# Attention weights times values: split fp32r products for two of four groups of key blocks, and another division of the column work between GpSimd and VectorE

## The chip, the cores and the metric

One core of a Trainium2 chip runs the whole program. The time is the device time of one execution in microseconds (us). TensorE (PE in the rows), VectorE (DVE), ScalarE (ACT), GpSimd (POOL) and the DMA queue of SyncE (SP) each work through an instruction list of their own, in order, and wait for each other on semaphores.

## What is computed

A two-layer encoder for 2048 prompt tokens and 256 sample tokens, width 1024, all in float32. Layer 0 is differential attention with 8 heads; layer 1 mixes by Fourier transforms. The change lies in layer 0, whose core is, for each head and each block of 128 queries:

```
s  = einsum(q, k) * scale - slope * |qpos - kpos|      # two maps m = 0, 1 per head, 2048 keys
p  = softmax(s)
pd = p[map 0] - lam * p[map 1]
o  = pd @ v                                            # v: 2048 keys x 128 columns
```

The 256 sample tokens attend among themselves in the same way.

## The kernel before

The program runs in stages: input projection, `attend`, output projection, then the three stages of the Fourier layer. `attend` is the second and longest one.

**Steps.** `attend` goes through 8 heads, and each head through 17 steps: q = 0 to 15 are the 16 blocks of 128 queries of the prompt, q = 16 is the sample. Every engine's list is written out by hand by its own `step(h, hs, q)`. A step of TensorE is: `half(0)`, `half(1)`, `turn(0)`, `pair(0)`, `turn(1)`, `half(2)`, `pair(1)`, `turn(2)`, `half(3)`, `turn(3)`, `pair(2)`, `pair(3)`.

**Scores.** `half(j)` writes 1024 columns of scores (map j // 2, half j % 2) to PSUM with fp32r matmuls (L1051, L1055, and L1054 for the diagonal block). Three score buffers (RING = 3) go round, so `half(1)` of a step waits for the exponential `exp(2)` of the step before. VectorE takes the maximum of each half (`maximum`, L1285) and, when both halves of a map are done, the scaled negative (`negative`, L1291). ScalarE then writes exp(scale * s - max) to `p0` (map 0) or `p1` (map 1) and the row sums (L1209).

**Combining.** One step later the two maps of a block become one set of weights, in place in `p0`. VectorE adds and inverts the row sums (`inverse_sums`, L1309 and L1312). GpSimd scales columns 0 to 1023 of `p1` by -lam / sum (L1377, signals `p1_scaled`), then columns 1024 to 2047 of `p1` (L1380), then the same columns of `p0` by 1 / sum (L1382), and adds the two (L1385, signals `weights_rest`). VectorE does columns 0 to 1023 with one instruction of two SBUF inputs (`combine`, L1323, signals `weights`); it stands last in VectorE's step.

**Turning.** A further step later `turn(c)` transposes 4 of the 16 key blocks of the weights (group c, 512 columns) with TensorE into the one PSUM buffer `turned` (L1085). ScalarE copies it to `wt` (`take_weights`, L1187), and the next `turn` waits for that copy. In steps 1 to 5 of a head there is a fifth turn, `turn_value` (L1094), for a part of v; it stands between `pair(2)` and `pair(3)`.

**Products.** `pair(x)` issues about a quarter of the step's products `vv[k] x wt[k]` (L1111), each 128 x 128 by 256 queries in float32; the trace shows each as two matmul instructions. A table (`QUARTERS`) spreads the 128 products of a head plus 2 of the sample over the 17 steps, in the order of k: 8 a step in most, two to each `pair`.

Of the kernel before, what the change touches and what calls it, by code (L numbers as in the profile page):

```python
# [60 lines left out]
def f32(ap):  # L61
    return ap.bitcast(F32)
# [720 lines left out]
def attend(nc, qk_hi, qk_lo, v_dram, o_dram, consts, lam_vectors, copies, first, rows, subln, ahead, ahead_branch, ahead_gate):  # L783
# [10 lines left out]
    SHORT, T0 = S_SAMPLE, S_PROMPT  # L794
    SCORES = 4 * NB + 2
    OUTS = NP + 1
    assert SCORES % RING == 0
    with ExitStack() as stack:
        m = Memory(nc, stack, "pa")

        ka = [first["ka"], m.sb("ka1", [P, 2, S], F32R)]
        kb = [[first["kb"], m.sb("kb01", [HD + ALIBI, S], F32R)],
              [m.sb(f"kb1{n}", [HD + ALIBI, S], F32R) for n in range(2)]]
        qa = [first["qa"], m.sb("qa1", [P, 2, PAIR], F32R)]
# [3 lines left out]
        vv = m.sb("vv", [P, NB + 2, P])  # L808
        p0 = m.sb("p0", [P, 4, S])
        p1 = m.sb("p1", [P, 2, S])  # L810
        wt = m.sb("wt", [P, 2, NB, PAIR])
# [23 lines left out]
        sq = m.sb("sq", [P, 2, 2, GROUP])  # L835
        row_w = m.sb("row_w", [P, 1])
        eps = m.sb("eps", [P, 1])
# [23 lines left out]
        turned_out = m.sem("turned_out")  # L861
# [6 lines left out]
        lam = load_lambda(m, m.sem("lam_in"))  # L868
# [70 lines left out]
        with nc.Block() as block:  # L939
            @block.sync  # L940
            def _(sp):
# [20 lines left out]
                def load_sample(h):  # L962
# [6 lines left out]
                    sp.dma_start(f32(diag_s[:]), row(consts["diag"], h, 0, P, 0, P)).then_inc(sample_in, 16)  # L969
# [64 lines left out]
            def _(pe):  # L1034
# [24 lines left out]
                def score_sample(h, n):  # L1059
                    no = 4 * NB + n  # L1060
                    if n == 0:
                        pe.wait_ge(sample_in, 144 * (h + 1))
                    wait(pe, exps, SCORES * h + no - RING + 1)
                    for b in range(2):
# [3 lines left out]
                        pe.matmul(out[:, at], ident_r[:], diag_s[:], start=False, stop=False)  # L1068
# [3 lines left out]
                def turn_weights(h, t, c):  # L1072
# [24 lines left out]
                def pair_product(h, q, quarter):  # L1097
                    for g, k, back in products_of[q][quarter]:
# [1744 lines left out]
```

## Time and profile before

| | us |
|---|---|
| median of 3 runs (2963.0 to 2968.81) | 2967.51 |
| the profiled execution's own time | 2963.53 |
| its span, first to last instruction | 2961.7 |
| mean granted TensorE clock | 0.981 |
| TensorE matmul busy, over the span | 2828.0 (95%) |
| VectorE, ScalarE, GpSimd busy | 1808.4, 1742.0, 1550.8 |
| in 1200 to 1400 us, inside `attend`: TensorE busy | 197.94 of 200 |
| the same stretch: VectorE, ScalarE, GpSimd busy | 144.58, 149.94, 124.87 |

The profile is one execution. `attend` runs from about 780 to 2050 us. Busy times of matmuls overlap, because matmuls are pipelined: what a matmul costs is the distance from its start to the next one's start. Idle time of an engine matters only where another engine waits at its end.

### The profile page before, as it was taken

The page shows a single profiled execution, that of the slowest core. Times are in us where ns is not written, and L with a number is a line of the kernel's source. Part 1 is how long each engine was busy: PE and PEld are TensorE (multiplying, and loading weights), DVE is VectorE, ACT ScalarE, POOL GpSimd, SP SyncE. Part 2 cuts the span into 40 slices and gives each one's busy share as a digit, 9 for nine tenths or more (in the row PEclk, how much of TensorE's full clock was granted, in tenths as well). Part 3 has the DMA queues.
Part 4 walks back from the last instruction along what each step waited for, and adds up shares of the span by engine and source line. Part 5 has one row for each costly group of instructions (what it writes and reads, how often), then busy time and mean ns, then how long its engine had stood idle before and what let it go on. Part 6 is the DMA issues. An engine that isn't in the chain of part 4 may idle for free. (4 is left out here: it accounts for less than half of the span.)

```text
span 2961.7 us, 41608 instructions
## 1 busy us (share of the span) xinstructions
PE 2828.0 (95%) x15126; PEld 2485.1 (84%) x15126; DVE 1808.4 (61%) x2402; ACT 1742.0 (59%) x3126; POOL 1550.8 (52%) x988
## 2 busy tenths in 40 slices
PE   5999999999799999999999999998999899899898
PEld 4999999999688787878788888886788899886687
DVE  7678668766576767777777777776886200441322
ACT  6777777767477777777777777775443311322321
POOL 4566655655366666666565666666664320230642
PEclk8999999999999999999999999999999999999899
DMA  3664554447452314141414131122565522565752
GB/s 113 186 198 136 175 172 149 151 145 205 125 178 77 95 29 107 36 109 36 106 31 109 36 88 56 31 91 87 193 206 174 176 90 78 159 171 197 257 193 99
DMA packets 281815, 374.02 MB, mean 126 GB/s; under 512 B 22923, under 2 KB 258507, under 8 KB 276140
## 3 DMA queue, kind: packets, MB, share of 16 engines
q1 hardware_dynamic: 281484, 371.23, 40.8%
q8 instruction: 121, 1.98, 0.3%
q14 instruction: 82, 0.67, 0.1%
q0 software_dynamic: 128, 0.13, 0.0%
HBM read 258.04 MB, written 125.97 MB: 130 GB/s over the span
## 5 line engine op out<-in xcount | busy, mean ns | idle before, releaser
L1285 DVE TENSOR_REDUCE pa_half_max<-pa_score 128x1 f32<-128x1024 f32 x512 | 623.9, 1219 | 322.6 <-PE pa_score L1055 322.5
L1209 ACT ACTIVATE pa_p<-pa_score,pa_neg_max 128x1024 f32<-128x1024 f32 x512 | 567.3, 1110 | 66.8 <-DVE pa_neg_max L1291 66.7
L1111 PE MATMUL pa_o_acc<-pa_wt,pa_vv 128*128 128x256 f32 x2048 | 513.9, 380 | 1.5 <-ACT pa_o_out_s L1248 1.5
L206 PE MATMUL ia_acc<-ia_xh,ia_wh 128*128 128x384 f32 x1344 | 454.3, 338 | 33.3 <-DVE ia_xl L675 15.9
L451 POOL TENSOR_TENSOR ia_w_sums<-ia_raw 128x512 f32<-128x512 f32 x240 | 334.1, 1395 | 256.2 <-PE ia_acc L208 236.3
L1051 PE MATMUL pa_score<-pa_ka,pa_qa 128*128 128x512 f32 x1024 | 453.0, 442 | 15.0 <-ACT pa_p L1209 8.0
L207 PE MATMUL ia_acc<-ia_xl,ia_wh 128*128 128x384 f32 x1344 | 452.3, 337 | 0.0
L208 PE MATMUL ia_acc<-ia_xh,ia_wl 128*128 128x384 f32 x1344 | 452.2, 336 | 0.0
L1187 ACT ACTIVATE pa_wt<-pa_turned 128x512 f32<-128x512 f32 x512 | 305.9, 597 | 241.7 <-PE pa_turned L1085 236.8
L1055 PE MATMUL pa_score<-pa_kb,pa_qb 96*128 96x512 f32 x1024 | 420.8, 411 | 0.0
L1111 PEld LDWEIGHTS pa_o_acc<-pa_wt,pa_vv 128*128 128x128 f32 x2048 | 366.2, 190 | 44.8 <-ACT pa_o_out_s L1248 3.1
L1377 POOL TENSOR_SCALAR pa_p<-pa_p,pa_inv_sum,pa_lam_neg 128x1024 f32<-128x1024 f32 x128 | 153.1, 1196 | 447.2 <-DVE pa_inv_sum L1312 447.2
L695 DVE TENSOR_TENSOR ia_c<-ia_c,ia_acc 128x384 f32<-128x384 f32 x384 | 199.0, 549 | 199.1 <-PE ia_acc L208 181.1
L1085 PE MATMUL pa_turned<-pa_ident,pa_p 128*128 128x128 f32 x2048 | 313.1, 275 | 3.9 <-ACT pa_wt L1187 3.6
L1385 POOL TENSOR_TENSOR pa_p<-pa_p 128x1024 f32<-128x1024 f32 x128 | 302.5, 2363 | 23.8 <-POOL pa_p L1382 23.8
L1085 PEld LDWEIGHTS pa_turned<-pa_ident,pa_p 128*128 128x128 f32 x2048 | 243.3, 140 | 77.6 <-ACT pa_wt L1187 39.4
L206 PEld LDWEIGHTS ia_acc<-ia_xh,ia_wh 128*128 128x128 f32 x1344 | 254.9, 190 | 39.2 <-issue 38.7
L207 PEld LDWEIGHTS ia_acc<-ia_xl,ia_wh 128*128 128x128 f32 x1344 | 254.7, 190 | 0.3
L208 PEld LDWEIGHTS ia_acc<-ia_xh,ia_wl 128*128 128x128 f32 x1344 | 254.8, 190 | 0.0
L1051 PEld LDWEIGHTS pa_score<-pa_ka,pa_qa 128*128 128x128 f32 x1024 | 195.5, 191 | 54.0 <-ACT pa_p L1209 14.9
L659 DVE TENSOR_TENSOR ia_wl<-ia_acc,ia_wh 128x512 fp32r<-128x512 f32 x336 | 225.8, 681 | 3.6 <-ACT ia_acc L565 3.1
L1055 PEld LDWEIGHTS pa_score<-pa_kb,pa_qb 96*128 96x128 f32 x1024 | 195.9, 191 | 33.4
(286 smaller groups left out, 5236.9 us busy)
## 6 DMA issues: line engine op xcount, KB each, us to landing
ia_raw<-attn_w_in SPq DMA_DIRECT2D x48, 1024.0 KB, 6.3
qk_hi<-ia_hi SPq DMA_DIRECT2D x96, 192.0 KB, 5.0
qk_lo<-ia_c SPq DMA_DIRECT2D x96, 192.0 KB, 3.0
pa_ka<-qk_hi SPq DMA_DIRECT2D x32, 512.0 KB, 9.0
fl_slices<-normed SPq DMA_DIRECT2D x26, 512.0 KB, 6.5
ia_h<-x_cols SPq DMA_DIRECT2D x24, 384.0 KB, 4.2
v<-ia_c SPq DMA_DIRECT2D x48, 192.0 KB, 5.6
attn_gate<-ia_c SPq DMA_DIRECT2D x48, 192.0 KB, 2.0
```

The costliest lines, as they stand in the source:

```text
L206: pe.matmul(out, a_hi(k), b_hi(k), start=first and n == 0, stop=False)
L207: pe.matmul(out, a_hi(k), b_lo(k), start=False, stop=False)
L208: mm = pe.matmul(out, a_lo(k), b_hi(k), start=False, stop=last and n == len(ks) - 1)
L451: pool.tensor_tensor(w_sums[:, s % RING], x, y, op).then_inc(w_sum, 1)
L1051: pe.matmul(out[:, c], qa[s][:, n, at:at + P], ka[hs][:, n, cols], start=True, stop=False)
L1055: mm = pe.matmul(out[:, c], qb[s][:, n, at:at + P], kb[hs][n][:, cols], start=False, stop=True)
L1085: mm = pe.transpose(turned[:, x * P:(x + 1) * P], src, ident[:])
L1111: mm = pe.matmul(acc, vv[:, k], wt[:, g % 2, k], start=k == 0, stop=k == NB - 1)
L1187: act.activation(wt[:, s, 4 * c:4 * c + 4, at:at + P], turned[:].rearrange("p (k t) -> p k t", k=4), ACT.Copy).then_inc(turned_out, 1)
L1209: act.activation(dst[:, half * HALF:(half + 1) * HALF], score[:, (4 * q + j) % RING].rearrange("p a b -> p (a b)"), ACT.Exp, bias=neg_max[ ...
L1285: dve.tensor_reduce(half_max[:, q % 2, n, half:half + 1], score[:, (4 * q + j) % RING].rearrange("p a b -> p (a b)"), AX_X, ALU.max).then_ ...
L1385: pool.tensor_tensor(b, b, p1[:, par, HALF:], ALU.add).then_inc(weights_rest, 1)
```

## The change

In `attend`, the key blocks of groups 1 and 3 (`LOW = (1, 3)`, 8 of the 16 blocks) no longer use one float32 product. Their turned weights and values are kept as a high part in fp32r and a remainder: `wt_hi`, `wt_lo`, `vv_hi`, `vv_lo`. Each product of such a block becomes three fp32r matmuls (hi x hi, hi x lo, lo x hi). ScalarE's copy writes the high part, as long as before; VectorE writes the remainder with a new instruction (`weights_low`, `v_low`: `turned` minus the high part, 512 columns, read from PSUM and SBUF). The next `turn` waits for this too (`low_out`), as `turned` is read twice.

The combining is divided anew: VectorE joins columns 0 to 511, GpSimd the other 1536. `combine` moves up in VectorE's step, behind `negative` of the first map, with `weights_low(1)` behind it; `weights_low(3)` and `v_low` stand last. `turn(1)` now waits for GpSimd's part, as `turn(2)` did, and so does `exp(2)` where `exp(3)` did. `turn_value` moves behind `pair(3)`. The sample's diagonal table is no longer loaded apart (8 small DMAs fewer), and some small buffers share memory.

```diff
@@ turn_weights, on TensorE
-                    if c == 2:
+                    if c == 1:
                         pe.wait_ge(weights_rest, NB * h + t - 1 if t >= 2 else NB * h)
                     wait(pe, turned_out, unit(h, t, "w", c))
+                    wait(pe, low_out, lows(h, t, "w", c))
@@ pair_product, on TensorE
-                            mm = pe.matmul(acc, vv[:, k], wt[:, g % 2, k], start=k == 0, stop=k == NB - 1)
+                            if is_low(k):
+                                at = low_at(k)
+                                pe.matmul(acc, vv_hi[:, at], wt_hi[:, g % 2, at], start=False, stop=False)
+                                pe.matmul(acc, vv_hi[:, at], wt_lo[:, g % 2, at], start=False, stop=False)
+                                mm = pe.matmul(acc, vv_lo[:, at], wt_hi[:, g % 2, at], start=False, stop=k == NB - 1)
+                            else:
+                                mm = pe.matmul(acc, vv[:, full_at(k)], wt[:, g % 2, full_at(k)], start=k == 0, stop=False)
@@ step, on TensorE
-                        turn_value(q - 1)
                         pair(3)
+                        turn_value(q - 1)
@@ exponential, on ScalarE
-                    if j == 3 and not (is_first(h) and q < 2):
+                    if j == 2 and not (is_first(h) and q < 2):
                         act.wait_ge(weights_rest, NB * h + (q - 1 if q >= 1 else -1))
@@ combine and the new instructions, on VectorE
-                    a, par = p0[:, (q - 1) % 4, :HALF], (q - 1) % 2
-                    dve.scalar_tensor_tensor(out=a, in0=a, scalar=inv_sum[:, par, 0:1], in1=p1[:, par, :HALF],
+                    a, par = p0[:, (q - 1) % 4, :GROUP], (q - 1) % 2
+                    dve.scalar_tensor_tensor(out=a, in0=a, scalar=inv_sum[:, par, 0:1], in1=p1[:, par, :GROUP],
                                              op0=ALU.mult, op1=ALU.add).then_inc(weights, 1)
+                def weights_low(h, t, c):
+                    dve.wait_ge(turned_out, unit(h, t, "w", c) + 1)
...
+                    dve.tensor_tensor(wt_lo[:, s, ks, at:at + P], turned[:].rearrange("p (k t) -> p k t", k=4),
+                                      f32(wt_hi[:, s, ks, at:at + P]), ALU.subtract).then_inc(low_out, 1)
@@ step, on VectorE
                             maximum(h, q, 1)
                             negative(h, q, 0)
+                        if parts["before"]:
+                            combine(h, q)
+                        low(1)
+                        if parts["score"]:
                             maximum(h, q, 2)
                             maximum(h, q, 3)
                             negative(h, q, 1)
-                    if parts["before"]:
-                        combine(h, q)
+                    low(3)
+                    if parts["score"] and (q, "v", q - 1) in place and q - 1 in LOW:
+                        v_low(h, q, q - 1)
@@ step, on GpSimd (HALF is 1024 columns, GROUP 512)
-                    pool.tensor_scalar(p1[:, par, :HALF], p1[:, par, :HALF], inv_sum[:, par, 1:2], lam["neg"][:, 0:1],
+                    pool.tensor_scalar(p1[:, par, :GROUP], p1[:, par, :GROUP], inv_sum[:, par, 1:2], lam["neg"][:, 0:1],
                                        ALU.mult, ALU.mult).then_inc(p1_scaled, 1)
-                    b = p0[:, (q - 1) % 4, HALF:]
-                    pool.tensor_scalar(p1[:, par, HALF:], p1[:, par, HALF:], inv_sum[:, par, 1:2], lam["neg"][:, 0:1],
+                    b = p0[:, (q - 1) % 4, GROUP:]
+                    pool.tensor_scalar(p1[:, par, GROUP:], p1[:, par, GROUP:], inv_sum[:, par, 1:2], lam["neg"][:, 0:1],
                                        ALU.mult, ALU.mult).then_inc(p1_rest, 1)
...
-                    pool.tensor_tensor(b, b, p1[:, par, HALF:], ALU.add).then_inc(weights_rest, 1)
+                    pool.tensor_tensor(b, b, p1[:, par, GROUP:], ALU.add).then_inc(weights_rest, 1)
```

VectorE's order in one step in the middle of a head, from the maximum of the first score half on. Before (x2 means twice in a row):

```order
L1285 TENSOR_REDUCE pa_half_max<-pa_score 128x1
L1309 TENSOR_TENSOR pa_row_sum<-pa_half_sum 128x2
L1312 RECIPROCAL pa_inv_sum<-pa_row_sum 128x2
L1285 TENSOR_REDUCE pa_half_max<-pa_score 128x1
L1291 TENSOR_SCALAR pa_neg_max<-pa_half_max 128x1
L1285 TENSOR_REDUCE pa_half_max<-pa_score 128x1 x2
L1291 TENSOR_SCALAR pa_neg_max<-pa_half_max 128x1
L1323 SCALAR_TENSOR_TENSOR pa_p<-pa_p,pa_inv_sum 128x1024
```

and now, where L1322, L1346, L1349, L1328 and L1360 are the former L1285, L1309, L1312, L1291 and L1323:

```order
L1322 TENSOR_REDUCE pa_half_max<-pa_score 128x1
L1346 TENSOR_TENSOR pa_row_sum<-pa_half_sum 128x2
L1349 RECIPROCAL pa_inv_sum<-pa_row_sum 128x2
L1322 TENSOR_REDUCE pa_half_max<-pa_score 128x1
L1328 TENSOR_SCALAR pa_neg_max<-pa_half_max 128x1
L1360 SCALAR_TENSOR_TENSOR pa_p<-pa_p,pa_inv_sum 128x512
L1368 TENSOR_TENSOR pa_wt_lo<-pa_turned,pa_wt_hi 128x4x128
L1322 TENSOR_REDUCE pa_half_max<-pa_score 128x1 x2
L1328 TENSOR_SCALAR pa_neg_max<-pa_half_max 128x1
L1368 TENSOR_TENSOR pa_wt_lo<-pa_turned,pa_wt_hi 128x4x128
```

The combining instruction, half as wide, has moved from the end to a place ahead of the two maxima of the second map; a remainder instruction (L1368) follows it, and another ends the step.

TensorE's order at the end of step q = 2, from `turn(3)` to the first score matmul of the next step. Before:

```order
L1085 MATMUL pa_turned<-pa_ident,pa_p 128x128 x4
L1111 MATMUL pa_o_acc<-pa_wt,pa_vv 128x256
L1094 MATMUL pa_turned<-pa_ident,pa_vt 128x128 x4
L1111 MATMUL pa_o_acc<-pa_wt,pa_vv 128x256
L1051 MATMUL pa_score<-pa_ka,pa_qa_51 128x512
```

and now (L1112 and L1122 are the former L1085 and L1094, L1077 the former L1051):

```order
L1112 MATMUL pa_turned<-pa_ident,pa_p 128x128 x4
L1143 MATMUL pa_o_acc<-pa_wt_hi,pa_vv_hi 128x256
L1144 MATMUL pa_o_acc<-pa_wt_lo,pa_vv_hi 128x256
L1145 MATMUL pa_o_acc<-pa_wt_hi,pa_vv_lo 128x256
L1143 MATMUL pa_o_acc<-pa_wt_hi,pa_vv_hi 128x256
L1144 MATMUL pa_o_acc<-pa_wt_lo,pa_vv_hi 128x256
L1145 MATMUL pa_o_acc<-pa_wt_hi,pa_vv_lo 128x256
L1122 MATMUL pa_turned<-pa_ident,pa_vt 128x128 x4
L1077 MATMUL pa_score<-pa_ka,pa_qa 128x512
```

The two products of this place, both of group 3, have become three matmuls each, and the turn of the values stands behind both instead of between them.

## Rows read from the trace of the kernel before

**Rows 1.** Timeline of one step: start, duration in us, engine, line [idle before, releaser].
```profile
1213.82 0.58 PE L1051 MATMUL pa_score<-pa_ka,pa_qa 128*128 128x512 f32 x1
...
1214.56 0.19 ACT L1209 ACTIVATION_READ_ACCUMULATOR pa_p<-pa_score,pa_neg_max 128x1 f32 x1
...
1214.80 0.19 PEld L1051 LDWEIGHTS pa_score<-pa_ka,pa_qa 128*128 128x128 f32 x1
...
1216.85 1.20 POOL L1377 TENSOR_SCALAR pa_p<-pa_p,pa_inv_sum,pa_lam_neg 128x1024 f32<-128x1024 f32 x1 [3.12 <-DVE pa_inv_sum L1312]
1217.27 0.42 PEld L1085 LDWEIGHTS pa_turned<-pa_ident,pa_p 128*128 128x128 f32 x4 [0.22 <-ACT pa_wt L1187]
...
1217.79 0.22 DVE L1291 TENSOR_SCALAR pa_neg_max<-pa_half_max 128x1 f32<-128x1 f32 x1
1217.97 0.60 ACT L1187 ACTIVATE pa_wt<-pa_turned 128x512 f32<-128x512 f32 x1 [0.75 <-PE pa_turned L1085]
...
1218.92 1.23 DVE L1285 TENSOR_REDUCE pa_half_max<-pa_score 128x1 f32<-128x1024 f32 x1 [0.91 <-PE pa_score L1055]
...
1219.37 0.57 PEld L1085 LDWEIGHTS pa_turned<-pa_ident,pa_p 128*128 128x128 f32 x4
...
1220.77 0.45 PE L1055 MATMUL pa_score<-pa_kb,pa_qb 96*128 96x512 f32 x1
...
1221.50 1.89 PE L1111 MATMUL pa_o_acc<-pa_wt,pa_vv 128*128 128x256 f32 x8
...
1222.52 0.21 DVE L1291 TENSOR_SCALAR pa_neg_max<-pa_half_max 128x1 f32<-128x1 f32 x1
...
1222.76 1.11 ACT L1209 ACTIVATE pa_p<-pa_score,pa_neg_max 128x1024 f32<-128x1024 f32 x1 [0.37 <-DVE pa_neg_max L1291]
...
1223.04 0.58 PE L1051 MATMUL pa_score<-pa_ka,pa_qa 128*128 128x512 f32 x1
```
**Rows 2.** Timeline, Fourier stage: first and twelfth of twelve fp32r matmuls of 256 columns.
```profile
2578.08 0.28 PE L206 MATMUL fl_ps<-fl_asn 128*128 128x256 f32 x1
...
2579.38 0.28 PE L208 MATMUL fl_ps<-fl_asn 128*128 128x256 f32 x1
```
**Rows 3.** Timeline, GpSimd and VectorE side by side in steps 16 and 1 of a head.
```profile
932.55 1.20 POOL L1377 TENSOR_SCALAR pa_p<-pa_p,pa_inv_sum,pa_lam_neg 128x1024 f32<-128x1024 f32 x1 [2.73 <-DVE pa_inv_sum L1312]
...
933.30 0.47 DVE L1299 TENSOR_SCALAR pa_neg_s<-pa_max_s 128x2 f32<-128x2 f32 x1
933.73 2.24 POOL L1380 TENSOR_SCALAR pa_p<-pa_p,pa_inv_sum,pa_lam_neg 128x1024 f32<-128x1024 f32 x1
933.78 1.28 DVE L1323 SCALAR_TENSOR_TENSOR pa_p<-pa_p,pa_inv_sum 128x1024 f32<-128x1024 f32 x1
...
953.55 2.35 POOL L1385 TENSOR_TENSOR pa_p<-pa_p 128x1024 f32<-128x1024 f32 x1 [0.18 <-POOL pa_p L1382]
...
954.88 2.11 DVE L1323 SCALAR_TENSOR_TENSOR pa_p<-pa_p,pa_inv_sum 128x1024 f32<-128x1024 f32 x1
```
**Rows 4.** Timeline, output projection: two VectorE and two GpSimd additions, all from SBUF.
```profile
2057.51 5.85 DVE L1806 TENSOR_TENSOR oa_wl<-oa_raw,oa_wh 128x1024 fp32r<-128x1024 f32 x2 [2.07 <-ACT oa_wh L1741]
...
2058.92 6.67 POOL L1596 TENSOR_TENSOR oa_wl<-oa_raw,oa_wh 128x1024 fp32r<-128x1024 f32 x2
```
**Rows 5.** Timeline of the first stage, then ns (min/median/max) of two lines of `attend`.
```profile
42.51 2.11 DVE L659 TENSOR_TENSOR ia_wl<-ia_acc,ia_wh 128x512 fp32r<-128x512 f32 x3
...
42.67 3.44 POOL L466 TENSOR_TENSOR ia_x_sums<-ia_hi,ia_h 128x1536 f32<-128x1536 f32 x1 [22.30 <-DVE ia_h L671]
...
L1318 DVE SCALAR_TENSOR_TENSOR pa_p_s<-pa_p_s,pa_inv_s x16: 475/478/483, 946.3 to 2032.4; 128x256 f32<-128x256 f32 x16
...
L1372 POOL TENSOR_SCALAR pa_p_s<-pa_p_s,pa_inv_s,pa_lam_neg x16: 550/554/556, 940.4 to 2031.4; 128x256 f32<-128x256 f32 x16
```
**Rows 6.** Timeline of TensorE: `turn_value` in steps 2 and 3 of a head.
```profile
963.99 0.66 PE L1094 MATMUL pa_turned<-pa_ident,pa_vt 128*128 128x128 f32 x4 [0.46 <-ACT pa_wt L1187]
...
973.47 0.66 PE L1094 MATMUL pa_turned<-pa_ident,pa_vt 128*128 128x128 f32 x4 [0.89 <-ACT pa_wt L1187]
```

More of the change, by code:

```diff
@@ L794, in attend @@
     SHORT, T0 = S_SAMPLE, S_PROMPT
+    LOW = (1, 3)
+    LOW_NB = 4 * len(LOW)
     SCORES = 4 * NB + 2
@@ L807, in attend @@
         vt = m.sb("vt", [P, T])
-        vv = m.sb("vv", [P, NB + 2, P])
+        vv = m.sb("vv", [P, NB + 2 - LOW_NB, P])
+        vv_hi = m.sb("vv_hi", [P, LOW_NB, P], F32R)
+        vv_lo = m.sb("vv_lo", [P, LOW_NB, P], F32R)
         p0 = m.sb("p0", [P, 4, S])
         p1 = m.sb("p1", [P, 2, S])
-        wt = m.sb("wt", [P, 2, NB, PAIR])
+        wt = m.sb("wt", [P, 2, NB - LOW_NB, PAIR])
+        wt_hi = m.sb("wt_hi", [P, 2, LOW_NB, PAIR], F32R)
+        wt_lo = m.sb("wt_lo", [P, 2, LOW_NB, PAIR], F32R)
         o_out = m.sb("o_out", [P, 2, PAIR])
@@ L834, in attend @@
         ones = m.sb("ones", [P, P])
-        sq = m.sb("sq", [P, 2, 2, GROUP])
-        row_w = m.sb("row_w", [P, 1])
-        eps = m.sb("eps", [P, 1])
+        small = m.sb("small", [P, 3])
+        row_w, eps = small[:, 0:1], small[:, 1:2]
         score = m.ps("score", [P, RING, 2, GROUP])
@@ L867, in attend @@
         pool_held, sp_held = m.sem("pool_held"), m.sem("sp_held")
-        lam = load_lambda(m, m.sem("lam_in"))
+        lam = load_lambda(m, m.sem("lam_in"), p_s_at, small[:, 2:3])
         order = []
@@ L881, in unit, with lows, is_low, full_at @@
             return UNITS * h + place[(t, kind, c)] - SKIPPED
+        low_order = [x for x in order if x[2] in LOW]
+        LOWS = len(low_order)
+        SKIPPED_LOWS = len(LOW)
+        def lows(h, t, kind, c):
+            return LOWS * h + sum(place[x] < place[(t, kind, c)] for x in low_order) - SKIPPED_LOWS
+        def is_low(k):
+            return k // 4 in LOW
+        def full_at(k):
+            return sum(not is_low(x) for x in range(k))
+        def low_at(k):
+            return sum(is_low(x) for x in range(k))
         def turned_block(t):
@@ L1067, in score_sample @@
                         pe.matmul(out, qa_s[:, n, at], ka_s[:, n], start=True, stop=False)
-                        pe.matmul(out[:, at], ident_r[:], diag_s[:], start=False, stop=False)
+                        pe.matmul(out[:, at], ident_r[:], diag[1][:], start=False, stop=False)
                         mm = pe.matmul(out, qb_s[:, n, at], kb_s[:, n], start=False, stop=True)
@@ L1091, in turn_v @@
                     wait(pe, turned_out, unit(h, t, "v", c))
+                    wait(pe, low_out, lows(h, t, "v", c))
                     for x in range(4 if c < NC else 2):
@@ L1104, in pair_product @@
                                 pe.wait_ge(turned_out, unit(h, 1, "w", 0) + 1)
-                            mm = pe.matmul(acc, vv[:, NB + k], wt_s[:, k], start=k == 0, stop=k == 1)
+                            mm = pe.matmul(acc, vv[:, full_at(NB + k)], wt_s[:, k], start=k == 0, stop=k == 1)
                         else:
@@ L1166, in step @@
                         pair(2)
+                        pair(3)
                         turn_value(q - 1)
-                        pair(3)
                     if is_last(h) and q == SAMPLE:
@@ L1339, in step @@
                             negative(h, q, 0)
+                        if parts["before"]:
+                            combine(h, q)
+                        low(1)
+                        if parts["score"]:
                             maximum(h, q, 2)
```

44 lines of the change are left out of this document (31 added, 13 removed).

## The prediction

> **What bounds the kernel now.** I read the page first: TensorE is 95% busy over the span, and the table by stretches gives it 197.94 of 200 us inside `attend`. A shorter product looks like a gain there. So I then walked through one step in the timeline [rows 1]. It lasts from the first score matmul at 1213.82 to the next at 1223.04: 9.22 us. Two chains run round in it, and the reader should see that both are full.
>
> The first is TensorE's own work, end to end. The second goes through the other engines. The last matmul of `half(3)` ends at 1221.22 (1220.77 + 0.45). VectorE's maximum of that half follows it, then the negative (1222.52 to 1222.73), and the exponential `exp(2)` (from 1222.76). The same exponential one step earlier ends with its accumulator read at 1214.75, and the weight load of `half(1)` starts at 1214.80. `half(1)` is thus released just in time. From there TensorE goes through `turn(0)`, `pair(0)`, `turn(1)`, `half(2)`, `pair(1)`, `turn(2)` and `half(3)`, and the ring is closed. Within it `turn(1)` waits as well: its weight load at 1217.27 has 0.22 us of idle ahead, ended by ScalarE's copy of `turn(0)`.
>
> **The products.** A float32 product is two matmuls: eight of them take 1.89 us [rows 1], which is (1.89 - 0.38) / 7 = 0.216 us apiece, or 0.432 for a product. Fp32r matmuls of 256 columns follow each other by (2579.38 - 2578.08) / 11 = 0.118 us [rows 2]; three make 0.354. A split product saves 0.078 us. There are 8 blocks x 8 pairs x 8 heads = 512 of them: 40 us of TensorE.
>
> By the table `QUARTERS` the split products of steps 5 to 14 lie in `pair(0)` and `pair(3)`, two in each. What `pair(0)` saves (0.16 us) is lost to `turn(1)`, which waits for the copy anyway. What `pair(3)` saves lies before `half(1)`, which is held by `exp(2)`: `half(0)` starts 0.16 us sooner, and `half(1)` waits. Hardly any of the 40 us reaches the end: the second ring has only the 0.05 us between 1214.75 and 1214.80 in it, and that is signal time. I take 0.
>
> **What is added to the second ring.** `turn(2)` must now wait for VectorE's remainder of `turn(1)`, which stands behind `combine`. When does `combine` run?
>
> GpSimd starts at 1216.85 [rows 1]. Its scaling takes 0.554 us for 256 columns [rows 5] and 1.20 for 1024 [rows 3], so 0.84 ns a column: 0.77 for 512 and 1.63 for 1536. It signals `p1_scaled` at 1217.62 and goes straight on with the 1536 columns, until 1219.25. VectorE finishes the negative at 1218.01 [rows 1] and comes to `combine` in the midst of this.
>
> Rows 3 show what happens then. The `combine` at 954.88 takes 2.11 us: GpSimd's addition runs until 955.90 (953.55 + 2.35), and `combine` ends 1.09 us later, at 956.99. In steps in which it starts clear of GpSimd it takes 1.28. At 933.78 it is the other way round: `combine` comes 0.05 us after a GpSimd scaling has begun, takes its normal 1.28 us, and the scaling takes 2.24 instead of 1.20. So the two exclude each other, and the later one waits for the whole instruction of the other. A small VectorE instruction at 933.30 lasts 0.47 us, until 933.77, and GpSimd's scaling ends at 933.75; a scaling excludes as well. Today `combine` stands last in the step, when GpSimd is nearly through and TensorE is not waiting.
>
> What the rows don't hold is a `combine` that begins in the middle of a scaling. The Trainium skill, page "SBUF — State Buffer", section "SBUF: two separate sides", covers it: a VectorE instruction with two SBUF inputs and a GpSimd instruction that reads SBUF share one port pair, an exclusive lock held for the whole instruction. By that rule the sum is the one below, 3080 us; if one held that a scaling lets `combine` in, it would be 2983. The trace agrees with the rule in all three places of rows 3.
>
> So `combine` gets going at 1219.25. A 512-column one is 0.53 us shorter than the 1.09, by (1.28 - 0.478) / 768 = 1.04 ns a column [rows 3, 5]: it ends at 1219.81. Does GpSimd's next queued scaling get in first? The nearest case is in the output projection: two VectorE additions (5.85 us) and two of GpSimd (6.67 us) started 1.41 us apart and went by turns [rows 4]; so one instruction is waited for, not two. The remainder takes 2.11 / 3 = 0.70 us, like the instruction of the first stage that also reads PSUM and SBUF; it ran beside a GpSimd addition of 3.44 us without being stretched [rows 5], so it needs no turn. ScalarE's copy, its input, is there at 1218.57 [rows 1]. It ends near 1220.42, and `turn(2)` loads weights at 1220.46. Today it loads at 1219.37 and could have done so about 0.15 later without loss: **0.95 us late**. As `half(0)` comes 0.16 us earlier than now, GpSimd's start moves with it, and 0.80 is left in steps 6 to 15. `half(3)`, the maximum, `exp(2)` and the next `half(1)` all move by this.
>
> Bounds: without exclusion `combine` ends at 1218.7 and the remainder at 1219.4, 0 late. With both scalings ahead of it, 1.63 later than mine. Within my case, scaling at a fixed rate per column (0.60 and 1.80 us) or a different spacing moves it by 0.15 either way.
>
> **Other edits.** GpSimd's additions of 1536 columns take 3.44 us [rows 5]; its step is 0.77 + 1.63 + 0.56 + 1.63 + 0.2 + 3.44 = 8.2 us of about 10, and its part arrives near 1225.1, before `turn(1)` at about 1227. No wait. `exp(2)`'s earlier wait is met likewise. `maximum(2)` starts up to 1.4 us later than 1218.92, but must only be done before `half(3)` is. The 8 sample DMAs fewer are behind other work: 0.
>
> `turn_value` (steps 1 to 5) now waits for the remainder of `turn(3)`, which stands behind the second negative. Today the wait is for ScalarE's copy alone: 0.46 us in step 2, 0.89 in step 3 [rows 6]. In steps 2 to 5 it starts 2.3 us after `half(3)` ends (0.04 + 1.22 + 0.25 for maximum and negative, 0.70 remainder, signals) instead of 1.4, less the product now ahead of it: 0.44, 0.95, 0.44, 0.46, together 2.3 us a head. In these four steps `half(0)` is not early, so the full 0.95 applies. Step 16: between `turn(1)` and `turn(2)` stand only the three products of `pair(2)`, two of them split (0.432 + 2 x 0.354 = 1.1 us), against copy plus remainder (1.4 us with signals): 0.3. Step 0: `combine` of the sample waits for GpSimd's longer addition: 0.4. Step 1: no `turn(1)`, four split products: -0.2.
>
> **The sum.** Per head 10 x 0.80 + 4 x 0.95 + 2.3 + 0.3 + 0.4 - 0.2 = 14.6 us; eight heads: 117. On the profiled execution's own 2963.5 us this is **3080**; it lies 4 us under the median shown, within the spread of the three runs.
>
> **Rivals.**
> - *Nothing blocks `combine`.* Then only the `turn_value` steps, step 16 and step 1 count: 2.4 x 8 = 19, so 2983 (2975 to 2990). Against it stand rows 3. Chance 0.09.
> - *Faster: the product saving arrives.* If `exp(2)` in truth leaves `half(1)` room, or the ring re-forms around TensorE, up to 40 us come through: 2923, or 2942 with the `turn_value` costs. It decides at a ring slack of more than 0.2 us a step; the 0.05 of rows 1 speaks against it, as does the copy wait at `turn(1)`. Chance 0.06.
> - *`combine` waits for both scalings.* Another 1.63 us in 14 steps, 8 heads: +180, so 3260. Rows 4 speak against it. Chance 0.04.
> - *The change doesn't shorten products* (a three-matmul product costs more than 0.354 because its weight loads show). Rows 2 have the same three-matmul form with a load each; and the ring would hide it. No case of its own.
>
> **How the numbers follow.** Main case 0.79, own range 3050 to 3115 (0.15 us x 14 x 8 = 17 us on either side, and as much again for the special steps). To leave out no more than 2 in 10 the range reaches down to the first rival: 2980 to 3115. A measurement of this kernel tells about 0.2% from no change, 6 us. Slower by more: main, first and third rival, 0.92; faster by more, the second, 0.06; within 0.2%: 0.02, where saving and waits cancel.
>
> **What would show it.** In a middle step, `combine` (512 columns) lasting about 1.8 us and ending 0.56 after a GpSimd scaling of 1536 columns; `turn(2)`'s weight load waiting for VectorE's remainder, some 0.8 to 1.0 us, over 100 times; a step of 10.0 us; products of split blocks 0.118 us apart; VectorE's remainders at 0.70 us. If `combine` takes 0.75 us and the step is still 9.2, the exclusion was misread. If the step is under 9.1, the second ring was.

## The result and the profile after

| | before | after |
|---|---|---|
| median, us | 2967.25 (2963.0 to 2968.81, 4 runs) | 3090.66 (3087.16 to 3094.91, 4 runs) |
| ratio to before, 95% interval | | 1.0418 [1.0406, 1.0431] |
| span of the profiled execution | 2961.7 | 3088.0 |
| VectorE busy | 1808.4 | 1998.5 |
| GpSimd busy | 1550.8 | 1797.0 |
| one step in the middle of a head | 9.22 | 10.04 |
| one head, median of the seven distances between heads | 155.8 | 169.9 |

The change costs 123.4 us. The last two rows are distances between starts of GpSimd's first scaling (L1377 before, L1439 after), which runs once in each step but that after the sample.

The table by stretches of the kernel after gives, for the same 200 us as in the table of before, the busy time of each engine, then granted clock, DMA share and GB/s:

```profile
core 0: us, PE busy (x) PEld busy (x) DVE busy (x) ACT busy (x) POOL busy (x), PEclk, DMA share, GB/s
1200.00:1400.00 200.00, 183.47 (x1073) 151.06 (x1072) 161.11 (x222) 137.62 (x254) 151.31 (x79) 1.00 0.22 60
```

TensorE was busy 197.94 of these 200 us, now 183.47, with the clock at full: it waits. The waits inside `attend` (engine, tile, line, what released it: us in total, times, longest) say for what. "issue" stands for idle time that no recorded event ended:

```profile
PEld pa_turned L1112 <- issue: 151.6, 238, 2.7
PE pa_turned L1112 <- DVE pa_wt_lo L1368: 82.7, 116, 2.3
...
PE pa_turned L1122 <- DVE pa_wt_lo L1368: 34.9, 32, 1.8
```

The turns wait for VectorE's remainder, `turn(2)` once in nearly every step and `turn_value` four times a head. The timeline of one middle step (start, duration, engine, line, [idle before, releaser]) answers to [rows 1]:

```profile
1409.99 0.77 POOL L1439 TENSOR_SCALAR pa_p<-pa_p,pa_inv_sum,pa_small 128x512 f32<-128x512 f32 x1 [1.96 <-DVE pa_inv_sum L1349]
...
1410.73 1.63 POOL L1442 TENSOR_SCALAR pa_p<-pa_p,pa_inv_sum,pa_small 128x1536 f32<-128x1536 f32 x1
1410.93 0.21 DVE L1328 TENSOR_SCALAR pa_neg_max<-pa_half_max 128x1 f32<-128x1 f32 x1
...
1411.06 1.84 DVE L1360 SCALAR_TENSOR_TENSOR pa_p<-pa_p,pa_inv_sum 128x512 f32<-128x512 f32 x1
...
1411.27 0.60 ACT L1225 ACTIVATE pa_wt_hi<-pa_turned 128x512 fp32r<-128x512 f32 x1 [0.76 <-PE pa_turned L1112]
...
1412.34 2.06 POOL L1444 TENSOR_SCALAR pa_p<-pa_p,pa_inv_sum,pa_ones 128x1536 f32<-128x1536 f32 x1
...
1412.82 0.68 DVE L1368 TENSOR_TENSOR pa_wt_lo<-pa_turned,pa_wt_hi 128x512 fp32r<-128x512 f32 x1
1413.42 1.21 DVE L1322 TENSOR_REDUCE pa_half_max<-pa_score 128x1 f32<-128x1024 f32 x1
1413.62 0.42 PEld L1112 LDWEIGHTS pa_turned<-pa_ident,pa_p 128*128 128x128 f32 x4 [0.99 <-issue]
1413.65 0.63 PE L1112 MATMUL pa_turned<-pa_ident,pa_p 128*128 128x128 f32 x4 [0.62 <-DVE pa_wt_lo L1368]
```

Read it from the middle. `combine` (L1360) starts at 1411.06, 0.33 us into GpSimd's scaling of 1536 columns, and lasts 1.84 us: it ends at 1412.90, 0.54 after the scaling (1410.73 + 1.63 = 1412.36). GpSimd's next scaling starts then too and takes 2.06 instead of 1.63: it waits in its turn. The copy of `turn(1)` (L1225) is there at 1411.87, but its remainder (L1368) runs only from 1412.82, and `turn(2)` loads weights at 1413.62 after 0.99 us of idle. In [rows 1] it loaded them 1.58 us after the negative started, now 2.69. This is nearly every step. The page's group (count | busy in all, mean ns | idle before) has a mean of 1.76 us, and of its 128 instructions 119 wait for GpSimd:

```profile
L1360 DVE SCALAR_TENSOR_TENSOR pa_p<-pa_p,pa_inv_sum 128x512 f32<-128x512 f32 x128 | 225.3, 1760 | 1.1 <-POOL pa_p L1439 1.1
```

### The profile page after: what moved, and what is told of

Its sections match the earlier page's. It is cut to its first block and busy times, and to the rows that moved or that the text cites. A ratio compares the mean times of both kernels' runs of the same rounds, so it can differ in the third digit from the quotient of the medians.

```text
span 3088.0 us, 43186 instructions
## 1 busy us (share of the span) xinstructions
PE 2841.8 (92%) x15638; PEld 2484.9 (80%) x15638; DVE 1998.5 (65%) x2674; ACT 1746.1 (57%) x3126; POOL 1797.0 (58%) x988
## 5 line engine op out<-in xcount | busy, mean ns | idle before, releaser
L1322 DVE TENSOR_REDUCE pa_half_max<-pa_score 128x1 f32<-128x1024 f32 x512 | 621.3, 1215 | 193.8 <-PE pa_score L1081 193.8
L1077 PE MATMUL pa_score<-pa_ka,pa_qa 128*128 128x512 f32 x1024 | 445.8, 435 | 14.3 <-ACT pa_p L1246 9.2
L1447 POOL TENSOR_TENSOR pa_p<-pa_p 128x1536 f32<-128x1536 f32 x128 | 444.9, 3476 | 23.8 <-POOL pa_p L1444 23.8
L1112 PE MATMUL pa_turned<-pa_ident,pa_p 128*128 128x128 f32 x2048 | 316.8, 277 | 89.5 <-DVE pa_wt_lo L1368 84.9
L1112 PEld LDWEIGHTS pa_turned<-pa_ident,pa_p 128*128 128x128 f32 x2048 | 234.7, 141 | 190.9 <-issue 152.4
L1225 ACT ACTIVATE pa_wt<-pa_turned 128x512 f32<-128x512 f32 x256 | 153.3, 599 | 279.3 <-PE pa_turned L1112 278.9
L1439 POOL TENSOR_SCALAR pa_p<-pa_p,pa_inv_sum,pa_small 128x512 f32<-128x512 f32 x128 | 98.3, 768 | 325.7 <-DVE pa_inv_sum L1349 325.7
L1147 PE MATMUL pa_o_acc<-pa_wt,pa_vv 128*128 128x256 f32 x1024 | 263.7, 380 | 0.0
L1444 POOL TENSOR_SCALAR pa_p<-pa_p,pa_inv_sum,pa_ones 128x1536 f32<-128x1536 f32 x128 | 259.6, 2028 | 0.0
L1077 PEld LDWEIGHTS pa_score<-pa_ka,pa_qa 128*128 128x128 f32 x1024 | 197.0, 192 | 62.7 <-ACT pa_p L1246 38.1
L1360 DVE SCALAR_TENSOR_TENSOR pa_p<-pa_p,pa_inv_sum 128x512 f32<-128x512 f32 x128 | 225.3, 1760 | 1.1 <-POOL pa_p L1439 1.1
```

What stands on the lines that cost most here:

```text
L1077: pe.matmul(out[:, c], qa[s][:, n, at:at + P], ka[hs][:, n, cols], start=True, stop=False)
L1112: mm = pe.transpose(turned[:, x * P:(x + 1) * P], src, ident[:])
L1147: mm = pe.matmul(acc, vv[:, full_at(k)], wt[:, g % 2, full_at(k)], start=k == 0, stop=False)
L1322: dve.tensor_reduce(half_max[:, q % 2, n, half:half + 1], score[:, (4 * q + j) % RING].rearrange("p a b -> p (a b)"), AX_X, ALU.max).then_ ...
L1444: pool.tensor_scalar(b, b, inv_sum[:, par, 0:1], ones[:, 0:1], ALU.mult, ALU.mult).then_inc(p0_rest, 1)
L1447: pool.tensor_tensor(b, b, p1[:, par, GROUP:], ALU.add).then_inc(weights_rest, 1)
```

## Experiments

Each ratio is to the kernel before on the same chip. Lengths of steps are read as above.

### Each part alone

`only_split`, against the kernel after (the waits for GpSimd's part go back to `turn(2)` and `exp(3)` as well):

```diff
-                        if parts["before"]:
-                            combine(h, q)
                         low(1)
...
                     low(3)
+                    if q != SAMPLE and parts["before"]:
+                        combine(h, q)
@@ combine and GpSimd: HALF for GROUP throughout
-                    a, par = p0[:, (q - 1) % 4, :GROUP], (q - 1) % 2
+                    a, par = p0[:, (q - 1) % 4, :HALF], (q - 1) % 2
...
-                    b = p0[:, (q - 1) % 4, GROUP:]
+                    b = p0[:, (q - 1) % 4, HALF:]
```

> One part alone: the split products, with their remainders on VectorE, the high parts from ScalarE, the sample's weights and the turn of v behind pair(3) as in the change; the division of the columns (1024 and 1024), the combining instruction at the end of VectorE's step and the waits of turn(2) and exp(3) are those of the kernel before. The remainder of turn(1) then stands directly behind the first negative, with nothing queued ahead of it that GpSimd can block. Theory: the remainders alone cost nothing in a middle step (0.68 us on VectorE, ended 0.1 us before turn(2) would start anyway), so the step stays at 9.22 to 9.35 us; the turns of v still cost their 2.3 us a head and the last stage of attend some 8 us, which makes 2967 + 18 + 8 = about 2990. Rival 1: the 40 us of cheaper products count as soon as the combining instruction is out of the way: 2950. Rival 2: the remainders and waits are dear by themselves, whatever stands behind the negative: 3050 or more.

Measured: 2998.7 us, 1.0107 [1.0092, 1.0122], 9 above the expectation. The middle step is 9.19; steps 2 to 5 take 10.95, 10.69, 11.61 and 9.18 in the second head, where the kernel before takes 9.27, 9.21, 9.80 and 9.70. So the remainders are free in a middle step. The excess lies at the turns of v, and part of it is TensorE's clock. In this head TensorE waits 1.82 us for a turn of v, until 980.96, and then its granted clock falls from 1.00 to about 0.5 (2.4 to 1.2 GHz) for 3.5 us. The third-last number of each row is the granted clock:

```profile
core 0: us, PE busy (x) PEld busy (x) DVE busy (x) ACT busy (x) POOL busy (x), PEclk, DMA share, GB/s
976.00:981.00 5.00, 3.18 (x19) 2.46 (x19) 4.13 (x7) 4.19 (x8) 4.82 (x4) 1.00 0.45 110
981.00:984.50 3.50, 3.50 (x11) 3.00 (x12) 1.69 (x2) 2.42 (x6) 0.07 (x1) 0.51 0.49 147
984.50:990.00 5.50, 5.50 (x32) 4.45 (x31) 4.08 (x7) 2.96 (x6) 4.14 (x4) 1.00 0.09 28
```

It falls so in four of the six heads between the first and the last, and they last 159.7 us. In the other two it stays at 1.00 after the same wait, and they last 158.1: 2.35 more than before, about the 2.3 expected. So a fall costs 1.6 us, and the four some 6 of the 31 us that this kernel loses. In the kernel before, where the longest such wait is 0.89 us, these heads show none. Why it falls in some heads only, no run shows.

`only_division` is the mirror image: the kernel before with those lines of the change alone.

```diff
@@ step, on VectorE, and GROUP for HALF in combine and on GpSimd
                             negative(h, q, 0)
+                        if parts["before"]:
+                            combine(h, q)
```

> The other part alone: float32 products throughout, as before, no remainders, the turn of v where it was; only the division of the columns is new (VectorE 512, GpSimd 1536), with the combining instruction behind the first map's negative and the waits of turn(1) and exp(2) on GpSimd's part. Theory: the combining instruction takes 1.8 us here too, since GpSimd's scaling of 1536 columns blocks it, but nothing of TensorE's ring stands behind it within the step but the maximum of half(2), whose score half ends later (half(2) ends about 2.3 us after the negative begins); the step stays within 0.15 us of 9.22 and the whole at 2967 to 2985. Rival: the block itself is what costs, through the maxima that stand behind it: a step of 9.6 us or more, 3020 and above.

Measured: 2977.0 us, 1.0031 [1.0019, 1.0043]. Its timeline has the same block:

```profile
1398.02 1.63 POOL L1383 TENSOR_SCALAR pa_p<-pa_p,pa_inv_sum,pa_lam_neg 128x1536 f32<-128x1536 f32 x1
...
1398.34 1.84 DVE L1323 SCALAR_TENSOR_TENSOR pa_p<-pa_p,pa_inv_sum 128x512 f32<-128x512 f32 x1
```

`combine` takes 1.84 us here as well, and the step 9.28: 0.06 more than before. Alone, the parts cost 31.4 and 9.7 us; together 123.4. **The 82 us between are neither part's own.** They need both the block on VectorE and a remainder behind it that TensorE waits for; the next runs take the two apart.

### The block

`hold_scaling`: GpSimd starts its 1536-column scaling only when `combine` is done, so that nothing of it runs beside `combine`.

```diff
                     b = p0[:, (q - 1) % 4, GROUP:]
+                    pool.wait_ge(weights, STEPS * h + q)
                     pool.tensor_scalar(p1[:, par, GROUP:], p1[:, par, GROUP:], inv_sum[:, par, 1:2], lam["neg"][:, 0:1],
```

> The changed kernel with one wait more: GpSimd starts its 1536-column scaling only when VectorE's combine is done. Nothing else is moved. Theory (the two exclude each other, and combine waits for the whole scaling): combine lasts 0.75 us instead of 1.84, turn(2) no longer waits, a middle step falls from 10.04 to about 9.25 us, the kernel to about 2990 us (3091 less 0.8 to 0.95 in 14 steps of 8 heads). What is left over the kernel before, some 20 to 25 us, is the waits of turn_value. Rival (the remainder instructions and their place in VectorE's order cost the time by themselves): no change, 3090, or slower, since GpSimd's part now comes 0.5 us later.

Measured: 3012.9 us, 1.0155 [1.0138, 1.0172]; the middle step falls from 10.04 to 9.26. Nothing was taken from any engine; GpSimd only got one more wait. The timeline:

```profile
1400.31 3.50 POOL L1448 TENSOR_TENSOR pa_p<-pa_p 128x1536 f32<-128x1536 f32 x1 [0.18 <-POOL pa_p L1445]
...
1403.37 0.45 DVE L1346 TENSOR_TENSOR pa_row_sum<-pa_half_sum 128x2 f32<-128x2 f32 x1
...
1404.24 0.77 POOL L1439 TENSOR_SCALAR pa_p<-pa_p,pa_inv_sum,pa_small 128x512 f32<-128x512 f32 x1 [0.43 <-DVE pa_inv_sum L1349]
...
1405.31 0.74 DVE L1360 SCALAR_TENSOR_TENSOR pa_p<-pa_p,pa_inv_sum 128x512 f32<-128x512 f32 x1
1405.97 0.68 DVE L1368 TENSOR_TENSOR pa_wt_lo<-pa_turned,pa_wt_hi 128x512 fp32r<-128x512 f32 x1
1406.15 1.62 POOL L1443 TENSOR_SCALAR pa_p<-pa_p,pa_inv_sum,pa_small 128x1536 f32<-128x1536 f32 x1 [1.14 <-DVE pa_p L1360]
```

`combine` takes 0.74 us, its unblocked length, and the remainder follows at once. But GpSimd is now a ring of its own: its addition (3.50 us, until 1403.81) holds up the sum of the rows, two columns wide (0.45 us instead of 0.15), which releases its next scaling 0.43 us after it fell idle. That ring is 9.26 us long, and in steps 2 to 5 (9.99, 10.10, 11.40, 9.61) the turns of v still wait. And in every head the granted clock falls to half for some 3.5 us behind a turn of v, as in `only_split`; the 11.40 us hold such a stretch. So the run stays some 20 us above the expectation, for reasons outside the block.

`scaling_in_two`: the 1536-column scaling issued as two of 768.

```diff
-                    pool.tensor_scalar(p1[:, par, GROUP:], p1[:, par, GROUP:], inv_sum[:, par, 1:2], lam["neg"][:, 0:1],
-                                       ALU.mult, ALU.mult).then_inc(p1_rest, 1)
+                    for at in (slice(GROUP, GROUP + 768), slice(GROUP + 768, S)):
+                        x = pool.tensor_scalar(p1[:, par, at], p1[:, par, at], inv_sum[:, par, 1:2], lam["neg"][:, 0:1],
+                                               ALU.mult, ALU.mult)
+                    x.then_inc(p1_rest, 1)
```

> The changed kernel with GpSimd's 1536-column scaling issued as two of 768 columns. Theory (an instruction is waited for whole, and the two engines go by turns): combine waits only for the first, 0.98 us instead of 1.63; it lasts about 1.2 us, a middle step about 9.4, the kernel 3020 us. Rival (combine waits until GpSimd has no further scaling queued, or for another reason than the instruction in flight): 3090 or a little more.

Measured: 3026.0 us, 1.0202 [1.0187, 1.0218]; step 9.40.

```profile
1410.07 2.38 POOL L1443 TENSOR_SCALAR pa_p<-pa_p,pa_inv_sum,pa_small 128x768 f32<-128x768 f32 x2
...
1410.39 1.20 DVE L1360 SCALAR_TENSOR_TENSOR pa_p<-pa_p,pa_inv_sum 128x512 f32<-128x512 f32 x1
```

`combine` waits for the first of the two only: 1.20 us, 0.64 less. With the same columns, the same bytes and one instruction more, the step is 0.64 us shorter. What counts is the length of the one instruction that is under way: `combine` waits 0.46 us instead of 1.10. A mere sharing of bandwidth would give no reason for this difference.

`combine_last`: `combine`, still 512 columns, moved behind the last remainder of VectorE's step.

```diff
-                        if parts["before"]:
-                            combine(h, q)
                         low(1)
...
+                    if q != SAMPLE and parts["before"]:
+                        combine(h, q)
```

> The changed kernel with VectorE's combine (still 512 columns) moved back to the end of VectorE's step, behind weights_low(3) and v_low. Theory (combine's place, in the midst of GpSimd's scaling, is what delays the remainder of turn(1)): weights_low(1) follows the negative at once, turn(2) doesn't wait, a middle step is about 9.25 us, the kernel 2990 us; combine waits for the addition of 1536 columns there, about 1.8 us, and nobody waits for it. Rival (VectorE's two remainders make it or the turned buffer the bound, wherever combine stands): 3090.

Measured: 3053.0 us, 1.0294 [1.0279, 1.0309], a clear miss; the middle step is 9.83.

```profile
1408.02 3.50 POOL L1447 TENSOR_TENSOR pa_p<-pa_p 128x1536 f32<-128x1536 f32 x1 [0.18 <-POOL pa_p L1444]
...
1409.64 2.42 DVE L1360 SCALAR_TENSOR_TENSOR pa_p<-pa_p,pa_inv_sum 128x512 f32<-128x512 f32 x1
...
1412.12 0.42 PEld L1112 LDWEIGHTS pa_turned<-pa_ident,pa_p 128*128 128x128 f32 x4 [0.69 <-DVE pa_p L1360]
```

Moved out of one GpSimd instruction, `combine` fell into a later one, the addition until 1411.52, and `turn(0)` waited 0.69 us. `turn(2)` no longer waits. The expectation looked only at the wait that was to go.

### Do cheaper products count?

`fewer_products`: the kernel before, without two of the eight products of each of the steps 5 to 14, one in `pair(0)` and one in `pair(3)`: 2 x 10 x 8 x 0.432 = 69 us of TensorE.

```diff
+                        if 5 <= q < NB - 1 and k in (5, 6, 12, 14):
+                            continue
```

> The kernel before, with two of the eight products of steps 5 to 14 left out, one in pair(0) and one in pair(3) (key blocks 5, 6, 12 and 14 are then missing from most outputs). That takes 2 x 0.432 us of TensorE's work out of 80 steps, five times what split products save there. Theory (a ring through the maximum, the negative and exp(2) holds half(1), and turn(1) waits for ScalarE's copy): the step stays at 9.2 us, the kernel at 2967, at most 5 less. Rival (TensorE's own work sets the step): 80 x 0.86 = 69 us less, 2898.

Measured: 2963.6 us, 0.9987 [0.9977, 0.9996]; step 9.18. TensorE's rows:

```profile
1369.37 0.19 PEld L1051 LDWEIGHTS pa_score<-pa_ka,pa_qa 128*128 128x128 f32 x1 [0.57 <-ACT pa_p L1211]
...
1371.81 0.42 PEld L1085 LDWEIGHTS pa_turned<-pa_ident,pa_p 128*128 128x128 f32 x4 [0.65 <-ACT pa_wt L1189]
```

`half(1)` now idles 0.57 us for `exp(2)`, and `turn(1)` 0.65 for the copy, where [rows 1] have nothing and 0.22. Of the 0.86 us left out of a step, 0.04 reached the end; the rest came back as waiting.

The other direction: put the split products where the second ring passes. `split_in_ring` does so in `split_v_moved` (below); `table_alone` makes the same edit in the kernel before, all products in float32.

```diff
-        QUARTERS = {4: (2, 2, 1, 1), **{q: (2, 2, 2, 2) for q in range(5, NB - 1)}, NB - 1: (2, 2, 2, 1),
-                    NB: (3, 3, 3, 2), 0: (2, 2, 2, 2), 1: (2, 2, 2, 2), 2: (2, 2, 1, 1), 3: (2, 2, 0, 0)}
+        QUARTERS = {4: (1, 1, 1, 1), **{q: (2, 2, 2, 2) for q in range(5, NB - 1)}, NB - 1: (2, 2, 2, 1),
+                    NB: (3, 2, 3, 3), 0: (2, 2, 2, 2), 1: (2, 2, 2, 2), 2: (2, 2, 2, 2), 3: (2, 2, 0, 0)}
```

> The run split_v_moved with another table of the products: step 4 takes 4 instead of 6 and step 2 of the next head 8 instead of 6 (the sample's step 3, 2, 3, 3), so that in steps 5 to 14 the four split products of a step lie in pair(0) and pair(1) instead of pair(0) and pair(3). pair(1) lies in the second ring (half(1), turn(1), half(2), pair(1), turn(2), half(3), maximum, negative, exp(2)). Theory of the rings: what pair(1) saves, 2 x 0.078 = 0.156 us a step, now counts; the step falls from 9.19 to 9.04 and the whole by about 80 x 0.156 = 12 us against split_v_moved, to 2955 to 2966. Rival: another ring (GpSimd's, or the wait for the remainder at turn(2)) stands right behind, and the time falls by less than 4 us.

> Control: the kernel before with nothing but the table of the products of split_in_ring; all products in float32. Each product costs the same here, so the rings stay as long as they are: 2967 within 3 us. Should it gain 5 us or more, the gain of split_in_ring is one of the table, not of the cheaper products.

Measured: `split_in_ring` 2995.7 us, 1.0100 [1.0085, 1.0116]; `table_alone` 2983.9, 1.0061 [1.0048, 1.0074]. Both miss, and for the same reason: a pair of query blocks now ends in the sample's `pair(1)`, and the next product waits for ScalarE to empty the accumulator:

```profile
1412.00 1.56 PE L1111 MATMUL pa_o_acc<-pa_wt,pa_vv 128*128 128x256 f32 x6 [1.87 <-ACT pa_o_out L1245]
```

(from `table_alone`), about 2 us a head. The control separates this: the table costs 16.8 us with float32 products (2983.9 - 2967.1) and 8.6 with split ones (2995.72 - 2987.15). So split products in `pair(1)` give some 8 us. Four medians stand in that figure, but the heads at full clock say the same: the table costs 1.7 us a head with float32 products (157.45 against 155.8) and 0.7 with split ones (157.60 against 156.9), so 1 us a head. The middle step goes from 9.19 to 9.12, while the control's stays at 9.22. Of the 0.156 us a step 0.07 arrive. What closes the ring at 9.12 is not shown; the next candidate is the remainder of `turn(1)` (1367.42 to 1368.11), which ends 0.12 us before `turn(2)` loads its weights:

```profile
1367.42 0.69 DVE L1369 TENSOR_TENSOR pa_wt_lo<-pa_turned,pa_wt_hi 128x512 fp32r<-128x512 f32 x1 [0.52 <-ACT pa_wt_hi L1226]
...
1368.23 0.42 PEld L1112 LDWEIGHTS pa_turned<-pa_ident,pa_p 128*128 128x128 f32 x4
```

### Can the split be had for less?

`hold_and_move_v`: `hold_scaling` with the turn of v behind `half(0)` of the next step. `split_v_moved`: the same move in `only_split`.

```diff
                     half(0)
+                    if parts["score"] and (q - 1, "v", q - 2) in place:
+                        turn_v(h, q - 1, q - 2)
...
-                        turn_value(q - 1)
@@ VectorE, instead of at the end of its step
                             maximum(h, q, 0)
+                            if (q - 1, "v", q - 2) in place and q - 2 in LOW:
+                                v_low(h, q - 1, q - 2)
```

> The change, with GpSimd's scaling of 1536 columns held until the combining instruction is done (as in the run hold_scaling, 3012.9), and with the turn of v moved: TensorE does it behind half(0) of the next step instead of at the end of its own step, and its remainder stands behind the first maximum of the next step instead of at the end of VectorE's step. Theory: turn(0) no longer waits for ScalarE's copy and VectorE's remainder of v at the step's end, so most of the 2.3 us a head that these turns cost goes; hold_scaling less some 15 to 18 us: about 2996. Steps 2 to 5 of a head then last 9.3 to 9.7 us instead of 10.0 to 11.4. Rival: what steps 2 to 5 lose is not the wait at the turn but VectorE's and ScalarE's added work in them; then the time stays within 5 us of 3013.

> The run only_split (2998.7 us) with the turn of v moved: TensorE does it behind half(0) of the next step, and its remainder stands behind the first maximum of the next step. In only_split the steps 6 to 14 of a head last 9.19 us, 0.03 less than before, and the whole excess sits in steps 2 to 5 (10.95, 10.7, 11.6, 9.2 against 9.3, 9.2, 9.8, 9.7). Theory: the turn of v at the step's end, with its remainder behind a combining instruction that waits for GpSimd's addition, is the cause, so with it moved steps 2 to 5 come within 0.2 us of those before and the whole to 2965 to 2978. Rival: added work of VectorE in these steps, 2985 or more.

Measured: `hold_and_move_v` 2995.1 us, 1.0091 [1.0074, 1.0108], as expected; `split_v_moved` 2987.2, 1.0067 [1.0054, 1.0080], 9 us above its range. In the first, steps 2 to 5 come to 9.36, 9.66, 9.81, 9.86, near those before. What is left is in part GpSimd's ring (9.26). A head is 2.3 us longer than before, 1.0 of it in steps 1 and 15, which took 8.80 and 8.83 before and now take 9.25 and 9.33. Of the 36 us by which the profiled execution is longer, 18 lie in the first seven heads; the rest lies ahead of the first scaling, in the last head and behind its last scaling. In the second they stay at 9.42, 10.14, 10.09, 10.34: the remainder of v now stands between `maximum(0)` and `turn(0)`, and `turn(0)` waits for it in the two steps of a head that have one. But the granted clock now stays at 1.00 in the heads after the first:

```profile
971.96 0.68 DVE L1375 TENSOR_TENSOR pa_vv_lo<-pa_turned,pa_vv_hi 128x512 fp32r<-128x512 f32 x1
...
972.78 0.63 PE L1112 MATMUL pa_turned<-pa_ident,pa_p 128*128 128x128 f32 x4 [1.20 <-DVE pa_vv_lo L1375]
```

`reordered`: `hold_and_move_v` with 768 / 1280 columns and `half(3)` ahead of `turn(2)`.

```diff
                         pair(1)
-                        turn(2)
                         half(3)
+                        turn(2)
+                        pair(2)
                         turn(3)
-                        pair(2)
                         pair(3)
@@ ScalarE
-                    take(2)
                     exp(1)
-                    take(3)
+                    take(2)
                     exp(2)
+                    take(3)
```

> The run hold_and_move_v with three more edits: the columns divided 768 to VectorE and 1280 to GpSimd, TensorE's step goes half(2), half(3), pair(1), turn(2), pair(2), turn(3), pair(3), and ScalarE does exp(1) before the copy of turn(2) and exp(2) before that of turn(3), outside the sample's step. The ring half(3), maximum, negative, exp(2), half(1) then no longer contains turn(2) and its wait for the remainder. Theory: with the ring shorter than TensorE's own work, the cheaper products begin to count, and the step falls to about 9.0 us: 2930 to 2965. Rival 1: GpSimd's own ring (its addition holds up VectorE's row sums, they release its next scaling) bounds at 9.2 us with 1280 columns: 2965 to 2985. Rival 2: the new order only moves the wait to the copies: 3000 or more.

Measured: 3039.5 us, 1.0243 [1.0227, 1.0258]; step 9.40, steps 2 to 5 about 11. ScalarE now takes `turn(3)` behind `exp(2)`, and VectorE, in order, can't begin the next step's maximum before that remainder:

```profile
1405.61 0.59 ACT L1226 ACTIVATE pa_wt_hi<-pa_turned 128x512 fp32r<-128x512 f32 x1
...
1406.23 0.69 DVE L1374 TENSOR_TENSOR pa_wt_lo<-pa_turned,pa_wt_hi 128x512 fp32r<-128x512 f32 x1 [1.76 <-ACT pa_wt_hi L1226]
```

Rival 2 of its expectation held. No version with split products beat the kernel before.

## Why the prediction was right

3080 was forecast; it came to 3090.7, inside the main case's range of 3050 to 3115.

- **The product saving is 0.** Shown by `fewer_products` (69 us less of products gave 4) and by the step of `only_split`, 9.19 against 9.22. The 0.05 us that the ring had room for is about what arrives.
- **`combine` waits for the whole scaling.** Forecast 1.8 us and an end 0.56 behind it; measured 1.84 and 0.54, in 119 of 128 cases; the other nine are told at the end. The rival in which nothing blocks it (2983) is out, and so is the one in which it waits for both scalings. `hold_scaling` and `scaling_in_two` show the block to be the cause of the long step, not only beside it.
- **The lateness of `turn(2)`.** Forecast 0.80 net for a middle step; measured 10.04 - 9.22 = 0.82.
- **The special steps.** In steps 2 to 5, 6.1 us a head were forecast (4 x 0.95 + 2.3); measured 1.82 + 1.70 + 1.30 + 0.98 = 5.80 (medians of the heads). Of these, TensorE's waits at the turns of v make 2.6 a head, (34.9 - 14.4) / 8, where 2.3 were forecast; 14.4 is the row of the kernel before:

```profile
PE pa_turned L1094 <- ACT pa_wt L1187: 14.4, 24, 0.9
```

  Steps 16 and 0 together were put at +0.7 and gave -0.1, step 1 at -0.2 and gave 0.05. Steps 6 to 15 gave 8.4 instead of 8.0. The sum of a head: 14.6 forecast, 14.1 measured; that it is so close is in part errors that cancel.
- **What the sum left out.** From the first head's first scaling to the last one's last the change costs 117.3 us, the figure of the forecast for eight heads, but only because the first head costs 17.9 (it has one step of 13.29 us). That is luck. Much of that long step, from 804.6 to 817.9, is TensorE at half clock, which the sum had no term for:

```profile
804.00:810.00 6.00, 5.22 (x20) 4.12 (x19) 4.67 (x7) 2.31 (x5) 5.19 (x4) 0.51 1.03 229
810.00:813.00 3.00, 1.38 (x9) 0.87 (x7) 2.45 (x4) 2.69 (x5) 2.66 (x1) 1.00 1.01 210
813.00:817.00 4.00, 3.80 (x13) 3.26 (x14) 1.52 (x3) 2.39 (x5) 0.00 (x0) 0.57 1.00 221
```

  Before, the clock is 1.00 from 802 to 817. The second slow stretch follows a wait of 1.82 us for the turn of v (0.69 before in this place). The first isn't tied to the change: `table_alone`, without a split product, has 0.53 from 799 to 810 and a step of 10.99 us there.
- **Outside the heads.** Another 9 us of span lie there. 0.8 come before the first scaling, where the kernels of this document differ by up to 4 us. 3.0 come at the end of `attend`: VectorE waits 2.78 us for the input of its last remainder, with the reciprocals that end the stage behind it, and TensorE idles 9.0 us ahead of the output projection's first matmul instead of 4.6. These 3.0 are the change's, and the sum had no term for them. The last 5.1 lie behind that matmul, where both kernels have the same code. This part takes 911.4 us now and 906.2 before, and 906 to 913 over the kernels of this document, 911.5 in `fewer_products`, which has no split product either. So it is scatter between executions.

## What to carry to other kernels

Where two engines exclude each other instruction by instruction, place a short instruction by what the other engine has under way at that moment, and ask who waits behind it: the same `combine` held to 1.84 us cost 10 us in all with nobody behind it and 82 us more with a remainder that TensorE needed. One semaphore wait on the engine that isn't in the ring gave 78 us back. And before a cheaper instruction is counted as a gain, leave that work out altogether: if the time stays, the engine is busy but not the bound. Last, read the granted clock before a step that is longer than its waits is explained: a 1.82 us wait of TensorE cost another 1.6 us where the clock fell behind it.

## What the runs showed of the hardware beyond what was expected

- The exclusion holds for tiny instructions too: VectorE's addition of 2 columns from two SBUF inputs took 0.45 us beside GpSimd's 1536-column addition and 0.15 clear of it (`hold_scaling`, after). VectorE's remainder, which reads PSUM and SBUF, took 0.675 to 0.693 us in all 256 cases of the kernel after, whatever GpSimd did beside it.
- In most cases the two engines go by turns: GpSimd's next scaling, already queued, let `combine` through first and took 2.06 instead of 1.63 us. So an instruction waits for the one under way, and for no second one. The Trainium skill, page "SBUF — State Buffer", section "SBUF: two separate sides", calls it an exclusive lock for the whole instruction, and the traces agree at 768, 1536 (scaling) and 1536 (addition) columns: waits of 0.46, 1.1 and 1.7 us.
- Which engine counts as under way can't be read from recorded starts that lie 0.05 us apart. In nine of the 128 steps, eight of them the sample's, `combine` starts 0.05 to 0.06 us after GpSimd's scaling, and it is the scaling that waits (2.14 us, and 0.75 for `combine`), as in the second case of [rows 3]; in one step at 0.06 us and in all later ones `combine` waits. `only_division` divides alike: `combine` goes first at 0.05 us and waits from 0.07 on. The prediction counted the case of [rows 3] as agreement: it shows the exclusion, but not that the first recorded start wins.

```profile
952.04 2.14 POOL L1442 TENSOR_SCALAR pa_p<-pa_p,pa_inv_sum,pa_small 128x1536 f32<-128x1536 f32 x1
952.09 0.75 DVE L1360 SCALAR_TENSOR_TENSOR pa_p<-pa_p,pa_inv_sum 128x512 f32<-128x512 f32 x1
```
